# Crossed 64x64 products between straight ones in the time mixer of a hybrid decoder block

## The reference, cut to what matters

```python
def step(S, inp):
    r_t, w_t, k_t, v_t, kk_t, a_t = inp
    sa = jnp.einsum('bhij,bhj->bhi', S, -kk_t)
    S = (S * w_t[:, :, None, :]
         + sa[..., None] * (kk_t * a_t)[:, :, None, :]
         + v_t[..., None] * k_t[:, :, None, :])
    y_t = jnp.einsum('bhij,bhj->bhi', S, r_t)
    return S, y_t
...
p = h @ w_in[l]          # (272, 2048) @ (2048, ...): r, k, v, pool and gate columns
```

## Time and profile before

| | us |
|---|---|
| median of 3 runs | 2401.98 (2398.24 to 2403.23) |
| the profiled execution | 2401.69 |
| its span, first to last instruction | 2399.8 |
| TensorE busy in the span | 2142.2 (89%) |

### The profile page before, as it was taken

How to read it: one execution, slowest core, us unless ns; L and a number is a source line. 1 busy time by engine, 2 the same in 40 slices (tenths; PEclk the granted TensorE clock), 3 DMA queues, 4 the chain that set the end, 5 groups by cost and what they waited for, 6 DMA issues and landing times.

```text
span 2399.8 us, 37842 instructions
## 1 busy us (share of the span) xinstructions
PE 2142.2 (89%) x15331; PEld 1505.0 (63%) x15331; DVE 1515.1 (63%) x2557; ACT 710.0 (30%) x1398; POOL 659.9 (27%) x540
## 2 busy tenths in 40 slices
PE   8999999999989999998998989878887787777776
PEld 8999999999889999987554444433332233222222
DVE  7778888888755555548887567667446444444445
ACT  6556555555244444432221111111011000000000
POOL 1000000000000000004555455555545445444442
PEclk9999999999999999999999999999999999999999
DMA  6533333333367666679999999999999999999997
GB/s 206 144 108 89 110 92 105 93 108 91 106 176 193 186 185 186 199 265 353 417 427 423 425 423 427 427 427 426 427 427 426 426 428 427 426 427 427 427 428 286
DMA packets 348321, 708.19 MB, mean 295 GB/s; under 512 B 13835, under 2 KB 272483, under 8 KB 281827
## 3 DMA queue, kind: packets, MB, share of 16 engines
q0 software_dynamic: 74176, 537.01, 53.2%
q1 hardware_dynamic: 273732, 168.55, 24.2%
q10 hardware_dynamic: 240, 0.22, 0.0%
HBM read 703.63 MB, written 2.10 MB: 294 GB/s over the span
## 4 chain that ended last, share of the span: by engine, by line
DMA 37%; PE 17%; issue 2%; DVE 2%; POOL 1%; DVEq 0%; ACT 0%; POOLq 0%; ACTq 0%
DMA query_w<-in_v_table,experts 15%; DMA rows<-in_v_table,experts 14%; PE bank L2003 7%; PE project L2003 3%; DMA down_row_more<-in_v_table,experts 3%; DMA up_rows<-in_u_table,experts 3%; DMA rows<-in_u_table,experts 3%; PE bank L247 2%; PE bank L1919 1%; PE project L247 1%; PE bank L1967 0%; PE bank L1635 0%; PE bank L1961 0%; POOL rows L1880 0%; PE bank L1946 0%
## 5 line engine op out<-in xcount | busy, mean ns | idle before, releaser
L2125 DVE CUSTOM_DVE_ANT_0 rows<-rows,h 128x2048 f32<-128x2048 f32 x170 | 388.6, 2290 | 329.2 <-DMA rows<-in_u_table,experts 328.9
L1874 POOL DMA_INDIRECT rows<-in_u_table,experts x170 | 185.0, 1088 | 1092.8 <-DVE experts L1472 1033.7
L232 DVE TENSOR_TENSOR w_half_rest<-w_half,w_half_high 128x1024 fp32r<-128x1024 f32 x224 | 272.8, 1219 | 156.1 <-ACT w_half_high L211 155.8
L247 PE MATMUL project<-hT_high,w_half_high 128*128 128x272 f32 (+1 forms) x1152 | 349.2, 303 | 6.3 <-DVE w_half_rest L232 6.0
L2003 PE MATMUL bank<-query_w,merged_spare 128*128 128x512 f32 x608 | 284.2, 604 | 60.0 <-DMA query_w<-in_v_table,experts 46.5
L2003 PE MATMUL bank<-rows,merged_spare 128*128 128x512 f32 x612 | 284.1, 601 | 57.6 <-DMA rows<-in_v_table,experts 44.2
L247 PE MATMUL project<-hT,w_half_high 128*128 128x272 f32 (+1 forms) x1152 | 330.1, 287 | 0.0
L247 PE MATMUL project<-hT_high,w_half_rest 128*128 128x272 f32 (+1 forms) x1152 | 329.1, 286 | 0.0
L2125 DVE CUSTOM_DVE_ANT_0 up_rows<-up_rows,h 128x2048 f32<-128x2048 f32 x86 | 196.9, 2290 | 169.5 <-DMA up_rows<-in_u_table,experts 169.5
L211 ACT CAST w_half_high<-w_half 128x1024 fp32r<-128x1024 f32 x224 | 234.7, 1051 | 228.9 <-PE merge_ps L247 116.1
L2003 PEld LDWEIGHTS bank<-query_w,merged_spare 128*128 128x128 f32 x608 | 112.3, 191 | 224.3 <-issue 122.9
(11 more groups left out here) (434 smaller groups left out, 3763.6 us busy)
## 6 DMA issues: line engine op xcount, KB each, us to landing
w_half<-in_w_in SPq DMA_DIRECT2D x176, 512.0 KB, 4.2
w_half<-in_w_branch_a SPq DMA_DIRECT2D x32, 512.0 KB, 4.0
out_w<-in_w_out SPq DMA_DIRECT2D x16, 1024.0 KB, 5.4
w_half<-in_w_branch_b SPq DMA_DIRECT2D x16, 512.0 KB, 4.0
query_w<-in_w_q_peer SPq DMA_DIRECT2D x8, 1024.0 KB, 16.4
out_w<-in_w_q_peer SPq DMA_DIRECT2D x6, 1024.0 KB, 21.2
lora_weights<-in_w_in SPq DMA_DIRECT2D x4, 896.0 KB, 14.0
rows<-in_u_table,experts POOLq DMA_INDIRECT x170, 21.1
```

The costliest lines, as they stand in the source:

```text
L232: return eng.tensor_tensor(low.bitcast(F32R), x, high, ALU.subtract)
L247: mm = nc.tensor.matmul(out, a.bitcast(F32R), b.bitcast(F32R), start=start and n == 0, stop=stop and n == 2)
L1874: pool.indirect_dma_start(ur[n % RU], None, w["u_table"][0], bass.IndirectOffsetOnAxis(ap=k.idx[:, t, h, j:j + 1], axis=0)).then_inc(s_u[n ...
L2125: v.tensor_tensor_reduce(ur[n % RU], ur[n % RU], k.h[:, n // (HEADS * TOPK), :], 1.0, 0.0, ALU.mult, ALU.add, dots(n, n + 1)).then_inc(s_d ...
```

## The change

The products that take a B-side tensor to or from the by-token side (`B_st` turned, the Gram matrices with B, the right-hand side, and what reads `U`) become calls of a new helper `crossed`. It uses the same operands, and writes the first head's result to partitions 64 to 127 and the second head's to 0 to 63. So the Gram matrix of A and B, its inverse, `RBKT_st` of B, B by token, the right-hand side and `U` hold their heads on exchanged halves, and the state and the outputs come back to their own halves, since the product that reads `U` is crossed again.

The number of head products stays the same. 30 of the 97 of a pair become crossed. `PE_ORDER` is rewritten: `t` is cut into `tk` (K), `tb` (B) and `tv` (V), `gr` into `gb` and `gk`, `Z` 5 and `T` 5 into single chunks (`Z5`, `T5`), the other `T` into all but the last two chunks and those (`Tl`), `s` into `kv` and `bu`, `r` into `mv`, and an output into `sv` and `ou`. Crossed entries are `rb`, `gb`, `tb`, `mv`, `sa`, `bu`, `ou`. `kv`, `sv` and `tk` get semaphores that TensorE itself waits for before a crossed product writes the same bank. In the long stretch `gb` alternates with `Z5`, and `tb`, `ou` and `mv` alternate with `T5` and `gk`; `rb` and `tv` open the next pass. In `ACT_ORDER` the rounding of weight half 2 moves from the long stretch to the start of the next pass, `lo` and `t` 1 change places, and `yc` goes behind `t` 0 and `r` 0. `DVE_ORDER` is unchanged.

```diff
 PE_ORDER = (
-    ("t", 1, 2), ("u", 0, 3), ("Z", 1, 2), ("f", 2, 0), ("gv", 0, 4), ("lw", 0, 1), ("f", 8, 0),
-    ("s", 0, 3), ("T", 1, 2), ("r", 1, 3), ("rk", 1, 2), ("sa", 1, 3), ("la", 0, 1), ("f", 6, 0),
-    ("u", 1, 3), ("T", 2, 2), ("s", 1, 3), ("r", 2, 3), ("rk", 2, 2), ("sa", 2, 3), ("lg", 0, 1), ("f", 10, 0),
...
-    ("u", 4, 3), ("Z", 5, 2), ("gr", 0, 1), ("s", 4, 3), ("T", 5, 2), ("t", 0, 1), ("gr", 1, 1), ("r", 0, 2), ("rb", 0, 1),
+    ("rb", 0, 2), ("tv", 0, 2), ("u", 0, 3), ("Z", 1, 2), ("f", 2, 0), ("gv", 0, 4), ("lw", 0, 1), ("f", 8, 0),
+    ("kv", 0, 3), ("rk", 1, 2), ("T", 1, 2), ("bu", 0, 3), ("Tl", 1, 2), ("mv", 1, 3), ("sa", 1, 3), ("la", 0, 1), ("f", 6, 0),
+    ("u", 1, 3), ("kv", 1, 3), ("rk", 2, 2), ("T", 2, 2), ("bu", 1, 3), ("sv", 1, 3), ("Tl", 2, 2), ("mv", 2, 3), ("sa", 2, 3), ("ou", 1, 3),
+    ("lg", 0, 1), ("f", 10, 0),
...
+    ("gb", 0, 1), ("Z5", 1, 2), ("gb", 1, 1), ("Z5", 2, 2), ("gb", 2, 1), ("Z5", 3, 2), ("gb", 3, 1), ("Z5", 4, 2), ("gb", 4, 1),
+    ("sv", 4, 3), ("u", 4, 3), ("tk", 0, 1),
+    ("T5", 1, 2), ("T5", 2, 2), ("T5", 3, 2), ("tb", 0, 1), ("T5", 4, 2), ("tb", 1, 1), ("gk", 0, 1), ("tb", 2, 1), ("gk", 1, 1), ("tb", 3, 1),
+    ("gk", 2, 1), ("ou", 4, 3), ("gk", 3, 1), ("mv", 0, 2), ("gk", 4, 1),
 )
 ACT_ORDER = (
-    ("lo", 0, 2), ("t", 1, 2), ("u", 0, 3), ("e", 2, 1), ...
+    ("t", 1, 2), ("lo", 0, 2), ("u", 0, 3), ("split", 2, 0), ("e", 2, 1), ...
...
-    ("u", 4, 3), ("split", 2, -1), ("yc", 0, 3), ("t", 0, 1), ("r", 0, 2),
+    ("u", 4, 3), ("t", 0, 1), ("r", 0, 2), ("yc", 0, 3),
 )
...
+        def crossed(out, wts, x, start=True, stop=True):
+            for h, o in zip(heads, heads[::-1]):
+                mm = nc.tensor.matmul(out[o], wts[h], x[h], start=start, stop=stop)
+            return mm
...
+            def gb(c, p, par):
+                if c == 0:
+                    wait(pe, q["st"], p + 1)
+                    wait(pe, q["off"], p)
+                mm = crossed(inv[0][:, c * CH:(c + 1) * CH], bst[:, c, :], ast[par][:, c, :])
...
+            def tb(c, p, par):
+                if c == 0:
+                    wait(pe, q["kturn"], p + 1)
+                mm = crossed(low[:, c * CH:(c + 1) * CH], bst[:, c, :], turn)
...
+            def mv(c, p, par):
...
+                mm = crossed(rhs_ps, mt[par][:, c, :], by_token(par, 2, c), stop=(c == 0))
...
             def sa(c, p, par):
                 wait(pe, q["S"], p * 4 + c)
-                by_head(rhs_ps, ast[par][:, c, :], s[c % 2], start=False).then_inc(q["rhs"], 1)
+                crossed(rhs_ps, ast[par][:, c, :], s[c % 2], start=False).then_inc(q["rhs"], 1)
...
-            def s_(c, p, par):
-                wait(pe, q["Uc"], p * 5 + c + 1)
-                if c < NCH - 1:
-                    if c == 0:
-                        wait(pe, q["off"], min(p + 2, PAIRS))
-                    by_head(s_ps, by_token(par, 1, c), by_token(par, 2, c), stop=False)
-                    by_head(s_ps, by_token(par, 0, c), u, start=False).then_inc(q["Snew"], 1)
+            def kv(c, p, par):
+                if c == 0:
+                    wait(pe, q["off"], min(p + 2, PAIRS))
+                by_head(s_ps, by_token(par, 1, c), by_token(par, 2, c), stop=False).then_inc(q["kv"], 1)
+            def bu(c, p, par):
+                wait(pe, q["kv"], p * 4 + c + 1)
+                wait(pe, q["Uc"], p * 5 + c + 1)
+                crossed(s_ps, by_token(par, 0, c), u, start=False).then_inc(q["Snew"], 1)
+            def sv(c, p, par):
...
+                y = y_ps[:, (c - 1) * CH:c * CH]
+                by_head(y, s[c % 2], rst[p % 3][:, c, :], stop=False)
+                by_head(y, by_token(par, 2, c), rbk[par][:, NCH - 2 + c, :], start=False, stop=False).then_inc(q["ysv"], 1)
+            def ou(c, p, par):
+                wait(pe, q["ysv"], p * 4 + c)
+                wait(pe, q["Uc"], p * 5 + c + 1)
+                crossed(y_ps[:, (c - 1) * CH:c * CH], u, rbk[par][:, c - 1, :], start=False).then_inc(q["Yo"], 1)
```

More of the change, by code:

```diff
@@ L819, in rk_ @@
                     wait(pe, q["Yc"], p - 1)
+                else:
+                    wait(pe, q["Yo"], (p - 1) * 4 + c - 2)
                 at = (c - 1) // 2 * (P + SEQ) + (c - 1) % 2 * CH
@@ L823, in rk_, with tk, tv @@
                     mm.then_inc(q["gram3"], 1)
[L825 to L835, removed]
+            def tk(_, p, par):
+                wait(pe, q["st"], p + 1)
+                for c in range(NCH - 1):
+                    mm = by_head(low[:, (NCH - 1 + c) * CH:(NCH + c) * CH], kst[par][:, c, :], turn)
+                mm.then_inc(q["kturn"], 1)
+            def tb(c, p, par):
+                if c == 0:
+                    wait(pe, q["kturn"], p + 1)
+                mm = crossed(low[:, c * CH:(c + 1) * CH], bst[:, c, :], turn)
+                if c == NCH - 2:
+                    mm.then_inc(q["tok_mm"], 1)
+            def tv(_, p, par):
+                wait(pe, q["vst"], p + 1)
+                wait(pe, q["tok"], p * 2 + 1)
+                for c in range(NCH):
+                    mm = by_head(low[:, c * CH:(c + 1) * CH], vst[:, c, :], center)
                 mm.then_inc(q["tok_mm"], 1)
             def Z(i, p, par):
-                if i == 0:
-                    return
                 if i == 1:
@@ L845, in Z, with Z5, step @@
                     wait(pe, q["X"], p * 2 + 2)
[L846 to L850 removed]
+                for c in chunks(i):
+                    mm = by_head(inv[2][:, c * HALF:(c + 1) * HALF], ltd[:, c, :], xs[:, c, :])
+                mm.then_inc(q["Z"], 1)
+            def Z5(c, p, par):
+                if c == 1:
+                    wait(pe, q["X"], p * 2 + 2)
+                    wait(pe, q["off"], p + 1)
+                mm = by_head(inv[2][:, c * HALF:(c + 1) * HALF], lto[:, c, :], xs[:, c, :])
+                if c == NCH - 1:
+                    mm.then_inc(q["Z"], 1)
+            def step(i, c):
+                if i in CARRIED:
+                    return by_head(inv[1][:, c * CH:(c + 1) * CH], zs[:, c, :], yz[:, :, c, :])
+                return by_head(inv[1][:, c * HALF:(c + 1) * HALF], zs[:, c, :], yb[:, c, :])
             def T_(i, p, par):
@@ L856, in T_, with Tl, T5 @@
                     wait(pe, q["rbr"], p + 1)
-                for c in chunks(i):
-                    if i in CARRIED:
-                        mm = by_head(inv[1][:, c * CH:(c + 1) * CH], zs[:, c, :], yz[:, :, c, :])
-                    else:
-                        mm = by_head(inv[1][:, c * HALF:(c + 1) * HALF], zs[:, c, :], yb[:, c, :])
-                mm.then_inc(q["WT"], 1)
-            def r_(c, p, par):
+                for c in chunks(i)[:-2]:
+                    step(i, c)
+            def Tl(i, p, par):
+                step(i, NCH - 2)
+                step(i, NCH - 1).then_inc(q["WT"], 1)
+            def T5(c, p, par):
+                if c == 1:
+                    wait(pe, q["Zst"], p * 5 + 5)
+                    wait(pe, q["Y"], p * LEVELS + 5)
+                mm = step(5, c)
+                if c == NCH - 1:
+                    mm.then_inc(q["WT"], 1)
+            def mv(c, p, par):
                 if c == 0:
```

41 lines of the change are left out of this document (17 added, 24 removed), and 8 rows, old and new, of tables (ACT_ORDER, PE_ORDER).

## The result

The changed kernel took 2408.67 us (median of 8 runs, 2405.91 to 2411.16), the kernel before beside it 2401.56 (8 runs): a ratio of 1.0028, interval 1.0018 to 1.0037. In a second set of 10 runs it took 2406.67 against 2402.0: 1.0021 (1.0012 to 1.003). So it is slower by 4.7 to 7.1 us, about the 0.2% (4.8 us) that was called the least this kernel can tell, and clear of the noise in both sets. The forecast was 2402.5; the range, 2397 to 2415, holds the result, the case's own range, 2400 to 2405, does not. The profiled execution took 2411.16, with a span of 2409.3. One run of a later experiment, e5_early_wait, took 7291.77 us, three times the others, for a reason that the record doesn't show; the ratio given there leaves it out.

A forecast was written before the change was run, and what follows sets the result against it. TensorE was taken as the bound, with VectorE's chain to `MT_st` limiting the long stretch's gain. Five stretches summed to +0.03 us a step, +0.5 over 16 steps on the median 2401.98: forecast 2402.5 us, range 2397 to 2415.

The forecast's parts named there:

- The price of a crossed product: TensorE time for a crossed product with straight ones on both sides: 0.014 us, between bounds of nothing and 0.117.
- The long stretch: Head products up to `Z` 1: `T` 5 ends at 1.93 us, `Z` 1 2.62 later; 5.49 becomes 5.25, -0.24 a step.
- signs of being wrong: Profile signs against the forecast: `T` 5 run ending before 1.8 us, or `Z` 1 within less than 2.6 us of it.
- the third rival: Crossed products cost nothing and start once their data are there: -0.27 us a step, 2397.7 us; chance 0.12.
- Chunk 0: Stretch of chunk 0: `bu` starts at 0.58 us, `sa` 0.70 later through VectorE's new state; 1.31 becomes 1.54, +0.23.
- Chunk 1: Stretch of chunk 1: `bu` after the copy of `U`, state, `sa`, then `ou`; 1.92 becomes 1.955 us, +0.03.
- chunk 3: Stretch of chunk 3: has the form of chunk 1's, taken as +0.03 us a step.
- chunk 2: Stretch of chunk 2: `bu` at 0.70 us, `sa` at 1.40, end 1.775 against 1.80, -0.02 a step.
- the three waits of TensorE for itself: Waits ahead of crossed products: covered, with 3 or more products between (0.35 us) against 0.33 needed, `kturn` barely.
- The sum: All five stretches of a step: -0.24 + 0.23 + 0.03 - 0.02 + 0.03 = +0.03 us, over 16 steps +0.5.
- the second rival: Half an overlap: the next straight load waits for the crossed one's second, 0.058 us each; +0.30 a step, 2406.8; chance 0.10.
- the no-overlap rival: A crossed product takes its full turn, 0.117 us: +0.71 a step, +11.4 in all, 2413 us; chance 0.25.

The follow-up runs named there:

- e5_early_wait: Changed kernel with the wait for `kv` put ahead of the last `T` product, not directly ahead of `bu`: 2406.66 us, 1.002 of the kernel before.
- e8: Changed kernel with one more VectorE operation of 128x320, result unused, ahead of the mask that makes `MT_st`: 2416.23 us (one run).
- e9: Changed kernel with two k-tiles of big products (`f` 2) moved from behind `Z` 1 to ahead of it: 2401.31 us, 0.9995 of the kernel before.
- e4: Changed kernel reordered: `kv` 0 behind `Z` 1, `bu` 0 ahead of `T`, `rk` 1 behind `Tl`, `ou` ahead of `sa` in chunks 1 to 3: 2397.83 us.
- e2: Changed kernel with all products straight again, new order kept: 2415.01 us, 1.0056 of the kernel before.
- second profile: Profile of the changed kernel run again without an edit: 2406.67 us (10 runs), 1.0021 of the kernel before.
- e10: e6 with two k-tiles of big products (`f` 2) moved from behind `Z` 1 to ahead of it: 2387.02 us, 0.994 of the kernel before.
- e7: Changed kernel with 17 head products (136 more TensorE records) ahead of the time mixer, into a bank overwritten later: 2413.76 us, 1.0052 of the kernel before.
- e6: Changed kernel with the order of e4 and the early `kv` wait of e5_early_wait in chunks 1 to 3: 2397.38 us, 0.9974 of the kernel before.
- e3: Changed kernel with 128 long-fulfilled waits added on TensorE ahead of the time mixer's products: 2412.05 us, 1.0041 of the kernel before.

## Why the prediction was right or wrong

- **The price of a crossed product** was taken as 0.014 and measured as nothing: pairs follow each other at 0.12 us, and `bu` 0 even starts ahead of the third `T` product in front of it. Of the two rules weighed there, the Trainium skill's page "TensorEngine Tiling (Array Packing)", Key Properties, agrees with the trace; that of "TensorE: Matmul & The Clock Gate", Part 3, The mechanism, as it was read there (loads on the same rows queue), does not: the trace has 0.12 for a pair.
- **The long stretch** was to change by -0.24 and changed by -0.41: `T` 5 ended at 1.79, not 1.93, because of that price (0.07) and of the round (0.06) that had been added for the first `gb`, and `Z` 1 came 2.58 behind it, not 2.62. By the letter both are signs of being wrong that the prediction named (before 1.8, within less than 2.6), but by 0.01 and 0.02 us, and e8 shows that VectorE's chain does hold `Z` 1. The step of the argument was right: the gain is cut off by VectorE's chain to `MT_st`. The wait was to be 0.7 to 0.9; the pause from `u` 0 to `Z` 1 is 0.73, of which the profile puts 0.42 down to `MT_st`. e8 and e9 show that nothing else holds `Z` 1. This stretch went as the third rival had it (-0.37, `T` 5 at 1.80).
- **Chunk 0**: +0.17 against +0.23. `bu` started at 0.42, not 0.58, again by the price; that the new state's chain then decides was right, the profile has `sa` waiting for `S`. But that chain took 0.80 where it was priced at 0.70, so two errors, 0.16 and 0.10, went against each other; why it is longer here is not shown. e4, with `bu` ahead of `T`, took 0.50 away.
- **Chunk 1** is the step that failed: +0.03 was forecast, +0.17 came. Missing were 0.09 for a second wait in front of `bu` (shown by e5 in chunks 2 and 3) and VectorE: it works from chunk 0's state to chunk 1's for 4.90 us without a pause, so the new state starts 1.38 behind `u`, and with `bu` earlier (e5) it stayed there. The chain was priced as if VectorE were free. In chunk 3 (+0.08 against +0.03) and chunk 2 (+0.02 against -0.02) the second wait, worth 0.08 there by e5, is enough for the difference. That the three waits of TensorE for itself are covered was thus wrong: the data are there in time, the instruction still costs.
- **The sum**, +0.03 a step, was right by luck, since errors cancel: -0.17 and -0.06 against +0.14, +0.05 and +0.04. The times are near the second rival's 2406.8, by luck as well: pairs 0.12 apart leave no room for its 0.058 a crossed product.
- **What was not seen** is what made the difference: all but 0.8 of the 4.7 to 7.1 us are in no regular step. The forecast multiplied one step by 16, and had no term for code coming in. Where two places fall into one stretch, TensorE reaches the second before its block is there: stops of up to 1.5 us in the changed kernel (1.65 in e5) where straight products in the same order had 0.5 to 0.7 (e2), and a low clock behind some of them. At the two places that e2 shares the packed stretch does not pass the 256 records between the two much faster (3.8 and 3.9 us, e2 3.9 and 4.0); what differs is that the transfer starts 2.7 to 3.0 us behind the first place where the stop is long, and 2.1 to 2.2 in e2. Added to that, the last pass, without another pair's products, shows the waits bare and lost 1.15 us (second profile) to the clock. The range held by luck: it had been drawn to the no-overlap rival, 2413, for another reason. That rival, with its products straight (e2), came to 2415.

Left open: why the transfer of a code block starts later in one execution than in the next (186 us: 2.74 and 1.71 us behind the first place), and later in the packed stretch than in e2; and why the clock holds behind a pause of 2.9 us in the kernel before and falls in the changed one. The moves in e4 were not run apart, though the stretches show those in chunk 0 and those in chunks 1 to 3 each. The order of e10 was not run with straight products, so what crossing gives in it is not shown.

## What to carry to other kernels

Products on crossed halves were free beside straight ones here, but they pay only as far as the next wait of the stretch: find the chain on the other engine that ends it, and put independent work ahead of the waiting product (e9; with the order and the early wait, e10: 0.6% faster than before, where the overlap alone was 0.2% slower). Price each extra wait in front of a product that sets a chain at 0.09 us. And if the regular step doesn't hold the loss, number an engine's instructions: a stop that moves when instructions are added far ahead, and that ends a fixed time behind the transfer of a code block, is code coming in.

## What the runs showed of the hardware

- TensorE stops behind record 192 of a block of 256, for up to 1.65 us, where the block's transfer of 16 KB ended too late: in 13 profiles it went on no earlier than 1.21 us after that end, and every stop of 0.5 us or more ended 1.21 to 1.53 us after it. The longer stops came where two such places lie in or just behind one dense stretch, the first 85 to 133 records into it, though not in each such stretch. One that comes earlier (first place 45, in the step of 569 us: 0.67 us from one product to the next) vanished in the wait for `MT_st` behind it. The Trainium skill, "Runtime: NRT & Kernel Launch", Instruction fetch mechanics, has code come in blocks of 256 instructions, which the trace bears out (123 transfers of 16 KB), and calls the cost of a block border mostly hidden; in the dense stretches here it is not.
- After a stop of 1.0 to 1.65 us the granted clock fell to 0.50 in some cases (186 us in the first profile; 153 and 500 us in e7; 286 us in e5) for 3.4 us, which cost another 1.4 to 1.6 us, or (454 us in e4, 284 us in e6) for 6.8 us, which cost 3.0; in others (464 us) it did not fall.
- A crossed product can start ahead of a straight one that stands before it in the order (at least 0.04 us in chunk 0).
- A fulfilled wait costs TensorE 7.48 us / 128 = 0.06 us in a row of waits (e3).
